# Feed-forward output: one 512-column matmul on the high weights instead of two of 256

## What is computed

```python
h = rmsnorm(x, norm_ffn[i])
gt, up = jnp.split(h @ w_ffn_in[i], 2, axis=-1)
x = x + (jax.nn.silu(gt) * up) @ w_ffn_out[i]
```

## Time and profile before

| what | value |
|---|---|
| median of 3 executions | 2224.82 us (2223.82 to 2225.35) |
| the profiled execution | 2224.25 us |
| its span, first to last instruction | 2222.4 us |
| mean granted clock of TensorE in it | 0.991 |
| TensorE busy | 2158.9 us, 97% |
| DVE busy | 1664.1 us, 75% |
| ACT busy | 1209.2 us, 54% |
| the four output stages, start of the first product to that of the last | 399.56 to 465.66, 839.17 to 901.53, 1494.42 to 1556.79, 2148.63 to 2210.99 us |

### The profile page before, as it was taken

How to read it: one execution, slowest core, us unless ns; L and a number is a source line. 1 busy time by engine, 2 the same in 40 slices (tenths; PEclk the granted TensorE clock), 3 DMA queues, 4 the chain that set the end, 5 groups by cost and what they waited for, 6 DMA issues and landing times.

```text
span 2222.4 us, 48626 instructions
## 1 busy us (share of the span) xinstructions
PE 2158.9 (97%) x19064; PEld 2098.9 (94%) x19064; DVE 1664.1 (75%) x2682; ACT 1209.2 (54%) x1831; POOL 0.3 (0%) x5
## 2 busy tenths in 40 slices
PE   7898999999899999999999999999999999999998
PEld 7888999999799999899999999999899999999998
DVE  8877877897948776788865787775687956877765
ACT  6446544456455445535746865444546747855444
POOL 0000000000000000000000000000000000000000
PEclk9999999999999999999999999999999999999999
DMA  5433565553445656564454455555554554455555
GB/s 213 141 127 107 178 206 183 182 175 129 134 143 175 215 187 198 178 194 149 150 181 144 132 181 196 195 188 200 184 182 143 169 172 133 136 194 184 188 185 166
DMA packets 104546, 378.67 MB, mean 170 GB/s; under 512 B 11584, under 2 KB 13760, under 8 KB 103872
## 3 DMA queue, kind: packets, MB, share of 16 engines
q1 hardware_dynamic: 103232, 370.77, 50.7%
q10 hardware_dynamic: 1152, 5.56, 0.7%
HBM read 375.23 MB, written 1.05 MB: 169 GB/s over the span
## 4 chain that ended last, share of the span: by engine, by line
PE 84%; DVE 10%; ACT 3%; issue 3%; DMA 0%; DVEq 0%; ACTq 0%
PE acc L655 23%; PE acc L656 23%; PE acc L657 23%; DVE w_lo L1635 3%; PE acc L759 1%; PE acc L760 1%; PE acc L761 1%; ACT w_hi L1189 1%; PE mid L1091 1%; PE acc L706 1%; PE acc L708 1%; PE acc L707 1%; PE mid L989 1%; PE mid L1074 1%; DVE pr L2349 0%
## 5 line engine op out<-in xcount | busy, mean ns | idle before, releaser
L1635 DVE TENSOR_TENSOR w_lo<-w_raw,w_hi 128x1024 fp32r<-128x1024 f32 x699 | 851.8, 1222 | 323.9 <-ACT w_hi L1189 315.7
L1189 ACT CAST w_hi<-w_raw 128x1024 fp32r<-128x1024 f32 x699 | 732.0, 1050 | 544.5 <-PE acc L657 500.7
L655 PE MATMUL acc<-h_hi,w_hi 128*128 128x256 f32 x2080 | 597.4, 287 | 11.4 <-DVE w_lo L1635 11.4
L656 PE MATMUL acc<-h_lo,w_hi 128*128 128x256 f32 x2080 | 585.9, 282 | 0.0
L657 PE MATMUL acc<-h_hi,w_lo 128*128 128x256 f32 x2080 | 585.8, 282 | 0.0
L655 PE MATMUL acc<-g_hi,w_hi 128*128 128x256 f32 x1488 | 419.9, 282 | 0.0
L656 PE MATMUL acc<-g_lo,w_hi 128*128 128x256 f32 x1488 | 418.1, 281 | 0.0
L657 PE MATMUL acc<-g_hi,w_lo 128*128 128x256 f32 x1488 | 418.0, 281 | 0.0
L655 PEld LDWEIGHTS acc<-h_hi,w_hi 128*128 128x128 f32 x2080 | 394.9, 190 | 20.9 <-DVE w_lo L1635 12.8
L656 PEld LDWEIGHTS acc<-h_lo,w_hi 128*128 128x128 f32 x2080 | 395.0, 190 | 0.4
L657 PEld LDWEIGHTS acc<-h_hi,w_lo 128*128 128x128 f32 x2080 | 394.8, 190 | 0.0
(11 more groups left out here) (439 smaller groups left out, 3420.6 us busy)
## 6 DMA issues: line engine op xcount, KB each, us to landing
w_raw<-weights_d SPq DMA_DIRECT2D x700, 512.0 KB, 3.4
p<-p_d ACTq DMA_DIRECT2D x3, 1080.0 KB, 8.2
rdec<-decay_d ACTq DMA_DIRECT2D x2, 768.0 KB, 5.0
p<-p_d SPq DMA_DIRECT2D x1, 1072.0 KB, 11.6
x<-x_d SPq DMA_DIRECT2D x2, 512.0 KB, 5.5
out_d<-work SPq DMA_DIRECT2D x4, 256.0 KB, 2.2
c<-c_d SPq DMA_DIRECT2D x1, 512.0 KB, 9.4
c<-c_d ACTq DMA_DIRECT2D x1, 448.0 KB, 10.1
```

The lines of the kernel that those rows point to most:

```text
L655: mm(dst, wh, hi[:, k, :], start=first and j == 0, stop=False)
L656: mm(dst, wh, lo[:, k, :], start=False, stop=False)
L1189: nc.scalar.copy(w_hi[:, slot, :], w_raw[:, slot, :]).then_inc(hi_done, 1)
L1635: tt(w_lo[:, slot, :], w_raw[:, slot, :], w_hi[:, slot, :].bitcast(F32), SUB).then_inc(lo_v, 1)
```

## The change

`f_hi` and `f_lo` become the two halves of one tensor `f_both`, at the same addresses. In the output stages a block of high weights is multiplied with both halves in one matmul of 512 columns: the product with the high activations falls into columns 0 to 255 of the bank, that with the low activations into columns 256 to 511. The product of the low weights with the high activations goes to columns 0 to 255 as before. So the bank holds the result in two parts, and DVE adds first the one and then the other to the residual, with a wait on its own first add between them. Slabs, ring, order and all other stages stay as they are.

```diff
-        f_hi = in_arena("f_hi", 0, [P, FF, T], F32R)
-        f_lo = in_arena("f_lo", 22528, [P, FF, T], F32R)
+        f_both = in_arena("f_both", 0, [P, 2, FF, T], F32R)
+        f_hi, f_lo = f_both[:, 0, :, :], f_both[:, 1, :, :]
...
+            def out_slabs(at, i, t, need):
+
+                bank(at, t)
+                both, first = acc[t % 4][:, :], acc[t % 4][:, 0:T]
+                for m in range(3):
+                    weights_of(at, i + m)
+                    slot = (i + m) % RING
+                    for k in range(m * KD, min(m * KD + KD, FF)):
+                        if need is not None:
+                            need(k)
+                        a = slice((k % KD) * P, (k % KD + 1) * P)
+                        mm(both, w_hi[:, slot, a], f_both[:, :, k, :], start=k == 0, stop=False, skip_group_check=True)
+                        done = mm(first, w_lo[:, slot, a], f_hi[:, k, :], start=False, stop=k == FF - 1, skip_group_check=True)
+                    done.then_inc(used, 1)
+
...
                 for n in range(KD):
-                    slabs_long(at, so + 3 * n, to + n, 3, FF, f_hi, f_lo, act_ready if n == 0 else None)
+                    out_slabs(at, so + 3 * n, to + n, act_ready if n == 0 else None)
...
                     wait_used(dve, at, so + 3 * n + 2)
-                    tt(x[:, n, :], x[:, n, :], acc[(to + n) % 4][:, 0:T], ADD).then_inc(out[(to + n) % 4], 1)
+                    tt(x[:, n, :], x[:, n, :], acc[(to + n) % 4][:, 0:T], ADD).then_inc(v_xhalf, 1)
+                    dve.wait_ge(v_xhalf, at.split * KD + (n + 1))
+                    tt(x[:, n, :], x[:, n, :], acc[(to + n) % 4][:, T:2 * T], ADD).then_inc(out[(to + n) % 4], 1)
                     if n:
                         residual(at, n - 1)
```

More of the change, by code:

```diff
@@ L465, in hybrid_kernel @@
         v_norm = sem("v_norm")
+        v_xhalf = sem("v_xhalf")
         gain_hi = sem("gain_hi")
```

## The result

| | before | after |
|---|---|---|
| median of 22 executions each | 2223.86 us | 2226.47 us |
| lowest to highest | 2220.71 to 2226.26 | 2223.56 to 2230.32 |
| ratio | | 1.0012, 95% interval 1.0007 to 1.0018 |

By this ratio the change makes the kernel slower by 2.7 us (1.6 to 4.0); the two medians differ by 2.6. The execution that was profiled took 2223.56 us, the lowest of its 22, and the profiled one of before, 2224.25 us, lies 0.4 us above the median of the 22; so the two spans are not subtracted here, the stretches inside them are. One execution of the kernel before, taken beside e12 to e14, took 3492.81 us at a mean granted clock of 0.557, and it is left out of every ratio and every mean here.

A forecast was written before the change was run, and what follows sets the result against it. It took TensorE's pace to bound the stages, with a short DVE chain at each end. Terms -2.32 + 0.10 + 0.08 + 0.23 + 4 x 0.46 = -0.07 us gave 2224.7 us, range 2220.0 to 2229.0.

The forecast's parts named there:

- Rival C: Behind the first stage's stall: a spell at clock 0.50 comes or goes, 1.3 us, giving 2223.4 or 2226.0; chance 0.16.
- Rival D: Output-stage matmuls: the 512 runs at twice 118.3 ns, so TensorE isn't shortened, 2227.0 us; chance 0.12.
- Part 1, TensorE: Output stages: each of 704 blocks goes from 354.9 to 351.6 ns, saving 2.32 us.
- rival A: Middle of each new matmul: the moving operand's break costs, 0.7 us per ns, 2231.7 at 10 ns; chance 0.06 past 6.4 ns.
- Part 2 in the first stage: The second tile's extra add delays a DVE subtraction by 0.23 us, all of it added to TensorE's 1.95 us stall.
- rival E: First output stage: DVE becomes the bound, all eight adds in the path, 2229.2 us; chance 0.04.
- Part 2 hidden: Stages from the second on: eight adds of 0.46 us fit into DVE's 24.7 us of waiting for ACT's casts.
- Four stage ends: At each output stage's end the second add lies in the path ahead of the mean, costing 0.46 us each time.
- Rival B: Matmul starts are worth more, at the narrow-weight pace: 7.0 instead of 2.3 us saved, 2220.0 us; chance 0.09.
- rival F: 512-column matmuls: load and matmul take 131 ns instead of 233.3, 72 us less, 2153 us; chance 0.01.

The follow-up runs named there:

- e12: Changed kernel with 96 unused semaphore increments (pads) in TensorE's first output stage, second sample; 2226.56 us against 2224.26 for the kernel before.
- e14: Changed kernel with 96 unused semaphore increments in TensorE's first output stage, third sample; 2225.54 us against 2224.26 for the kernel before.
- e9: Changed kernel with both activation halves of each block side by side, so the 512-column operand is one run; 2225.91 us against 2223.72 before.
- e1: Changed kernel without DVE's second add, TensorE's part alone; 2223.75 us against 2224.55 for the kernel before.
- e2: Kernel before with DVE's add done twice, first into a scratch row, DVE's part alone; 2227.98 us against 2224.55 before.
- e13: Changed kernel unaltered, measured a third time; 2226.15 us against 2224.26 for the kernel before.
- e6: Kernel before with 256 unused semaphore increments in TensorE's first output stage, a whole instruction transfer, as control; 2224.94 us against 2224.16.
- e5: Kernel before with 160 unused semaphore increments in TensorE's first output stage, shifting instruction transfer boundaries; 2224.47 us against 2224.16.
- e10: Changed kernel unaltered, measured a second time; 2225.36 us against 2223.72 for the kernel before.
- e7: Changed kernel with 96 unused semaphore increments in TensorE's first output stage, restoring instruction transfer boundaries; 2225.56 us against 2224.16 for the kernel before.
- e4: The change in the second, third and fourth output stages only, the first as before; 2224.45 us against 2224.55 for the kernel before.
- e8: Changed kernel with the old form in each stage's last tile and the first stage's second tile, 8 pads; 2222.55 us against 2224.16 before.
- e11: Old form in each stage's last tile and the first stage's second tile, activation halves side by side; 2222.73 us against 2223.72 before.
- e15: Changed kernel with the old form in the first output stage's second tile only; 2226.66 us against 2223.78 for the kernel before.
- e18: Changed kernel with the old form in the first output stage's last tile only, second sample; 2224.71 us against 2223.78 for the kernel before.

## Why the prediction was wrong

The prediction called a time within 0.2% the likeliest, which it is, but by a sum of -0.07 us, no change at all. The measured change is +2.7 us (1.6 to 4.0), above that sum by more than the measurement is uncertain. That 2226.5 lies in the stated range is due to the range's width, and that it lies near two of the rivals' times (C's 2226.0, D's 2227.0) is luck, for neither's mechanism is what happened. Step by step:

- **Part 1, TensorE: right in kind, mis-sized.** The step that failed is "233.3 + 118.3 = 351.6 ns". It added two paces, each read where the same kind follows itself; in turn they give 353.2. Forecast -2.32 us, measured 704 x 1.75 = -1.23. This is 1.1 us of the miss, and it is the term of the sum that was wrong, not a cost of the split operand: the guess "I take nothing for it" held (e9), so rival A falls. A stage is 0.30 us shorter and not 0.58. The one row of a 512 behind a 256 that the prediction looked at, printed to 0.01 us, was too coarse to see 1.6 ns.
- **Part 2 in the first stage: right.** Subtraction 0.23 us later, as forecast; the stall +0.33, which the sum had as +0.23 and +0.10 for the blocks that reach it sooner. (That second part alone isn't seen: in e1, with the faster blocks and one add, the stall is 2.00 us, inside the 1.95 to 2.05 of the old form.) No later wait for low weights came up there, so rival E falls.
- **Part 2 hidden: right.** In the later stages no wait of TensorE for low weights appeared; they last 62.06 us with the second add and 62.07 without it (e1).
- **Four stage ends: right.** 0.46 us each. The last product and the mean are 3.06 us apart at the first end before and 3.53 after; the stretches between the stages from the second on went from 592.89 to 593.36 and from 591.84 to 592.30, that at the end from 11.44 to 11.88. In e1, without the second add, they are 592.95, 591.89 and 11.45, and in e2, with the old matmuls and two adds, the first two are 593.37 and 592.34: the cause is shown. "0.9 instead of 0.4" and "2.8 instead of 2.35" were met by 0.88 and 2.81.
- **Rival D,** the 512 at twice 118.3 (236.6 ns), gave 2227.0, near the measured time, but not for its reason: 234.6 ns lies between its figure and the forecast's 233.3, and TensorE's part is shorter, by 1.23 us.
- **Rival B** (starts worth more than the rows say) and **rival F** fall with the same 234.6. The Trainium skill's sustained 131 ns for 512 columns (TensorE: Matmul & The Clock Gate, Back-to-back issue gap) isn't met by this form of matmul; the section's other figure, 512 / 2.4 + 2.5 = 216 ns, isn't either.
- **Rival C, the clock: it comes and goes, in the old form and in the new.** The spell at 0.50 behind the stall is there in the profiles of before and after and not in that of e13, the same kernel as after; it is there in e6 and not in e5, both the kernel before with pads. These are the stretches (columns as in the earlier trace rows) that begin 1.6 us behind the stall's end in the changed kernel, and 2.5 us behind it in e13, where the clock is 1.00 in between as well:

```profile
425.90:429.30 3.40, 3.40 (x12) 2.92 (x11) 3.33 (x10) 0.65 (x1) 0.00 (x0) 0.51 0.81 287
```

```profile
429.30:432.70 3.40, 3.40 (x21) 2.99 (x20) 3.31 (x12) 2.12 (x4) 0.00 (x0) 1.00 0.82 257
```

The first output stage lasts 66.1 us with it (the changed kernel, e10) and 64.6 without (e7, e13): 1.5 us, beside the 1.3 that was worked out. Over the executions of the kernel before beside the experiments, the medians of those with a mean granted clock of 0.992, 0.991, 0.990 and 0.989 (29, 72, 36 and 14 of them) are 2223.1, 2223.9, 2224.8 and 2225.7 us. So a part of the scatter of a single time is such spells. They don't make the difference between the two kernels: over 45 executions of the changed kernel (its 22, e10, e13) the medians at 0.992, 0.991 and 0.990 (6, 21 and 15 of them) are 2225.5, 2225.6 and 2226.3 us, at the same mean clock 1.4 to 2.4 above.

What is shown of the cause, then: with the pace at its measured size the sum is +0.9 us, a loss, since the four seams (+1.84) and the stall (+0.33) cost more than the 704 starts return (-1.23). What stays open: three comparisons of the changed kernel gave +2.6, +1.6 and +1.9 us by the medians, +2.7, +1.1 and +1.3 by the ratio, so 0.2 to 1.8 above the terms, and only the first of the three is clear of them by its interval. If there is a rest, it lies ahead of the second stage, for behind it the seven profiles with the new form in all stages have the +0.5 of the terms (+0.46 to +0.52 over the profile of before, of which -0.9 are the pace and +1.4 the seams). Ahead of it the profiles don't show it: those seven start their second stage at 839.6 us in the mean, the four with the first stage in the old form (before, e4, e5, e6) at 839.2, 0.3 us apart where the terms have 0.5, with a scatter of over 1 us.

Of the causes that could stand behind a rest, the layout is not one (e9), and more frequent spells at the lower clock are not either as far as the runs show: at the same mean clock the distance stays, the mean clock of e10 and e13 differs by less than 0.0001 from that of the kernel before beside them, and the seven profiles spent 31.2 us at 0.50 ahead of the second stage against 34.1 us in the four. The moved transfers may hold a part of it, but no 1.2 us showed (e7, e12, e14). It was not seen where the first stage is in the old form (e4) or both of its sensitive tiles are (e8, e11), and e15 to e18 didn't tie it to one of the two; all of these are comparisons that can't tell 1 us. The cause of what is left over stays open.

## What to carry to other kernels

Merging two matmuls of 256 columns into one of 512 saves a start, here 1.8 ns of 355, and no column; any work that the merged result needs on another engine must be hidden everywhere, and at a seam where TensorE waits for that engine one more 0.46 us step outweighs 260 saved starts (0.46 / 0.00175). If such a change is made, the seams can keep the old form: by the profiles e8 and e11 kept most of the gain and dropped the price, and their medians, 1.6 and 1.0 us under the kernel before, agree with that without proving it. And when a term is a difference of a few ns times hundreds, read the pace of the very sequence that will run; two paces each read among their own kind don't add up to it.

## What the runs showed of the hardware

- A 512 and a 256 in turn take 353.2 ns with 128x128 weights at a granted clock of 1.00, 1.6 ns more than the 233.3 and 118.3 that each takes among its own kind; a moving operand in two runs of 256, 22,528 bytes apart, costs nothing measurable against one run of 512 (62.17 us for 176 blocks both ways).
- Two adds of DVE with a wait on the first start 0.45 us apart (411.71 and 412.16), an add and the independent step behind it 0.34 (412.16 and 412.50): by these two pairs the wait on its own result costs DVE some 0.11 us. The Trainium skill (VectorE: DVE Perf Modes, The DRAIN you can't avoid) has it that a semaphore after each operation costs nothing extra; in this trace, where the second step waits on the one ahead, the two starts lie further apart than without a wait.
- Work added or removed on TensorE far upstream moves its waits for instructions: "issue" 2.0 us at one product of the second layer in the changed kernel, 1.8 us inside a burst ahead of it with 96 pads. In total time the move was worth less than could be measured.
- Behind the last output stage TensorE idles 2.35 to 2.81 us ahead of the mean, and its clock falls at times before the mean begins: its two matmuls take 0.70 us at 1.00 (e11) and 1.22 us at 0.50 (e2, e8).
